# Skipped expert pairs counted before the used ones: blocks numbered from the end, norm work split four and four

## The reference

```python
def modulated_norm(x, g, shift, scale):
    return rmsnorm(x, g) * (1 + scale) + shift

def hierarchical_moe(h, wg, bg, we, be, w1, w3, w2):
    pg = softmax(x @ wg + bg);  pg_sel, g_sel = top_k(pg, 1)          # one of 4 groups
    le_sel = (x @ we + be) of that group                              # 4 experts in it
    w_top, i_top = top_k(softmax(le_sel), 2)                          # two experts
    w_top = w_top / sum(w_top) * pg_sel
    hid = silu(x @ w1[e]) * (x @ w3[e]);  y = sum_e gates[e] * (hid @ w2[e])
```

## Time and profile before

| | us |
|---|---|
| median of 3 runs | 2230.29 (2224.9 to 2230.62) |
| profiled execution, its own time | 2219.47 |
| its span in the trace | 2217.3 |
| PE busy | 1915.4 (86%) |
| DVE busy | 896.2 (40%) |
| ACT busy | 481.3 (22%) |
| POOL busy | 373.1 (17%) |

### The profile page before, as it was taken

One profiled execution on the slowest core, in us unless ns is written; L12 is line 12 of the kernel. 1 busy time (PEld: TensorE's weight loads), 2 busy tenths in 40 slices (PEclk: granted clock), 3 DMA queues, 4 the chain that ended last, 5 costly groups with the idle time before them and its releaser, 6 DMA issues. The chain is left out here.

```text
span 2217.3 us, 24642 instructions
## 1 busy us (share of the span) xinstructions
PE 1915.4 (86%) x9669; PEld 1300.0 (59%) x9669; DVE 896.2 (40%) x1686; ACT 481.3 (22%) x810; POOL 373.1 (17%) x280
## 2 busy tenths in 40 slices
PE   3899978978888895899679999888888889599975
PEld 2455655558888754444345566556888865444433
DVE  2179014565555424011237920546555541311114
ACT  1211013351111213122131101344111120322212
POOL 0001150043433102100111000005444300300001
PEclk8999897999999997899789999899999999699996
DMA  9322896800000003999562112530000000499953
GB/s 358 41 75 82 278 290 209 298 1 1 1 1 1 10 2 129 354 364 365 218 161 76 38 57 77 197 126 1 1 1 1 1 12 0 168 383 358 372 226 121
DMA packets 113920, 302.54 MB, mean 136 GB/s; under 512 B 27904, under 2 KB 35746, under 8 KB 100642
## 3 DMA queue, kind: packets, MB, share of 16 engines
q1 hardware_dynamic: 65424, 218.73, 26.7%
q0 software_dynamic: 14080, 53.48, 7.3%
q10 hardware_dynamic: 34322, 28.99, 4.6%
HBM read 235.09 MB, written 67.05 MB: 136 GB/s over the span
## 5 line engine op out<-in xcount | busy, mean ns | idle before, releaser
L626 PE MATMUL ps<-hreg,ring 128*128 128x512 f32 x768 | 400.2, 603 | 7.7 <-ACT hreg L1141 7.7
L627 PEld LDWEIGHTS ps<-hreg,ring 128*128 128x128 f32 x768 | 147.8, 192 | 187.6 <-issue 187.6
L986 PE MATMUL ps<-ring,tok 128*128 128x512 f32 x544 | 237.9, 595 | 0.2 <-issue 0.2
L986 PEld LDWEIGHTS ps<-ring,tok 128*128 128x128 f32 x544 | 103.9, 191 | 130.9 <-issue 130.9
L627 PE MATMUL ps<-hreg,ring 128*128 128x128 f32 x768 | 149.0, 276 | 0.0
L1969 POOL TENSOR_TENSOR hreg<-hreg,cst 128x512 f32<-128x512 f32 x70 | 88.9, 1270 | 301.7 <-DVE hreg L1674 254.7
L1001 PE MATMUL ps<-ring,work 128*128 128x512 f32 x272 | 123.7, 598 | 0.0
L626 PEld LDWEIGHTS ps<-hreg,ring 128*128 128x128 f32 x768 | 118.8, 195 | 8.0 <-issue 8.0
L1881 DVE TENSOR_TENSOR work<-work,ps 128x256 f32<-128x256 f32 x34 | 14.2, 421 | 252.5 <-ACT work L1364 252.5
L1503 DVE SCALAR_TENSOR_TENSOR mixA<-cin_reg,small,mixA 128x655 f32<-128x655 f32 x120 | 107.0, 895 | 0.0
L1687 DVE TENSOR_TENSOR hreg<-hreg,ps 128x512 f32<-128x512 f32 x50 | 34.3, 687 | 164.9 <-PE ps L846 164.9
(11 more groups left out here) (358 smaller groups left out, 3306.5 us busy)
## 6 DMA issues: line engine op xcount, KB each, us to landing
ring<-in_w SPq DMA_DIRECT2D x102, 1024.0 KB, 8.2
ring<-in_w_mod SPq DMA_DIRECT2D x24, 2048.0 KB, 8.6
ring<-in_w_in SPq DMA_DIRECT2D x12, 2048.0 KB, 9.0
ys<-zs ACTq DMA_DIRECT2D x34, 512.0 KB, 7.8
tok<-xs SPq DMA_DIRECT2D x30, 512.0 KB, 11.0
xs<-zero POOLq DMA_DIRECT2D x8, 1792.0 KB, 19.6
ys<-zero POOLq DMA_DIRECT2D x8, 1664.0 KB, 18.6
ring<-in_w_out SPq DMA_DIRECT2D x4, 2048.0 KB, 8.1
```

What stands on the lines that cost most here:

```text
L626: mm(o[:, 0:TS], lhs(k), rhs(k)[:, 0:TS], start=k == 0, stop=k == nk - 1)
L627: ins = mm(o[:, TS:T], lhs(k), rhs(k)[:, TS:T], start=k == 0, stop=k == nk - 1)
L986: ins = mm(bank(2 + q), xgT[q][:, k, :], w, start=k == 0, stop=k == KD - 1)
```

## The change

Four things are done.

1. The experts' blocks are shifted behind the unused ones: with skip = 26 - 2 x (used pairs), each slot moves up by 128 x skip rows and each expert's end by skip blocks. In every engine's loop the branch is turned round: pairs below skip / 2 raise their semaphores, the rest do the work. In SP's loop, which starts at pair 1 and has a limit of its own (skip + 2), the raises have lost their waits.
2. The norm's eight chunks are split four (DVE) and four (POOL), and all of DVE's stand ahead of the selection. ACT takes the chunks in order.
3. The bias row is spread over all partitions by two small products in the output projection (m == 2) and copied by DVE (m == 3); the logits then need one product per chunk, and DVE adds the bias as it reads them.
4. Block 1 is turned into other PSUM banks (`turn_block(1, 2048)`), without the wait for ACT's copy of block 0.

The second block's expert is computed for itself (entry NBLK + 2 of `blocks`). The order of the transfers in SP's and POOL's streams is the same in both kernels.

```diff
-                e = sp.value_load(blocks[0:1, 1:2], min_val=0, max_val=NE - 1)
+                e = sp.value_load(blocks[0:1, NBLK + 2:NBLK + 3], min_val=0, max_val=NE - 1)
                 up_load(1, e)
                 down_load(1, e)
                 need(xs_written, 16 * 2 * NCH)
-                in_use = sp.value_load(blocks[0:1, NBLK:NBLK + 1], min_val=1, max_val=NBLK)
+                unused = sp.value_load(blocks[0:1, NBLK + 1:NBLK + 2], min_val=2, max_val=NBLK + 2)
                 with sp.Fori(1, NPAIR) as pr:
-                    with sp.If(pr * 2 < in_use):
+                    with sp.If(pr * 2 < unused):
+                        for q in range(2):
+                            sp.sem_inc(ring_loaded[q], 32)
+                            sp.sem_inc(w2_loaded[q].sem, 16)
+                            sp.sem_inc(xg_loaded[q].sem, 16)
+                    with sp.Else():
...
-                need(xg_copied, 1)
                 need(xf_loaded[1], 16)
-                turn_block(1)
+                turn_block(1, 2048)
...
-                with act.Fori(0, NPAIR) as pr:
-                    with act.If(pr * 2 < in_use):
-                        pair(pr)
-                    with act.Else():
+                with act.Fori(0, NPAIR) as pr:
+                    with act.If(pr * 2 < unused):
                         for sig, n in ((sil_ready, 0), (xg_copied, 2), (hid_copied, 0)):
                             wait(pr, sig, n, 2)
                             act.sem_inc(sig.sem, 2)
                         for q in range(2):
                             wait(pr, ys_stored[q], 0, 16)
                             act.sem_inc(ys_stored[q].sem, 16)
+                    with act.Else():
+                        pair(pr)
...
-                norm_one(0)
+                for k in range(4):
+                    norm_one(k)
...
-                norm_one(1)
-
...
-                V.tensor_copy(slots[:, :], sl).then_inc(slots_ready.sem, 1)
...
+                step(V.tensor_tensor(t3, end[:, NE - 1:NE].to_broadcast([P, NPAIR]),
+                                     cst[:, C_BLK:C_BLK + NBLK].rearrange("p (n a) -> p a n", a=2)[:, 0, :], ALU.is_gt))
+                step(V.tensor_reduce(used, t3, AX, ALU.add))
+                step(V.tensor_scalar(skip, used, -2.0, float(NBLK), ALU.mult, ALU.add))
+                V.tensor_scalar(bf[:, NBLK + 1:NBLK + 2], skip, 2.0, None, ALU.add)
+                step(V.tensor_scalar(used, skip, float(P), None, ALU.mult))
+                V.tensor_scalar(slots[:, :], sl, used, None, ALU.add).then_inc(slots_ready.sem, 1)
+                step(V.tensor_scalar(wide_[:, 32:32 + NE], end, 1.0, None, ALU.is_le))
+                step(V.tensor_reduce(bf[:, NBLK + 2:NBLK + 3], wide_[:, 32:32 + NE], AX, ALU.add))
+                step(V.tensor_scalar(end, end, skip, None, ALU.add))
...
-                for k in range(2, KD):
+                for k in range(4, KD):
                     G.tensor_tensor(hT[:, k, :], xT[:, k, :], rst, ALU.mult).then_inc(norm_xp.sem, 1)
```

More of the change, by code:

```diff
@@ L212, in build @@
         crow = work[0:2, 512:532]
+        crb = work[:, 752:852].rearrange("p (c n) -> p c n", c=NCH)
         route_c = work[:, 544:544 + NX]
@@ L538, in _ @@
                             down_load(q, experts[q])
-                    with sp.Else():
-                        for q in range(2):
-                            sp.wait_ge(ring_loaded[q], up_base[l][q] + pr * 32)
-                            sp.sem_inc(ring_loaded[q], 32)
-                            sp.wait_ge(w2_loaded[q].sem, w2_loaded[q].at(l, 0) + pr * 16)
-                            sp.sem_inc(w2_loaded[q].sem, 16)
-                            sp.wait_ge(xg_loaded[q].sem, xg_loaded[q].at(l, -16) + pr * 16)
-                            sp.sem_inc(xg_loaded[q].sem, 16)
             sp.wait_ge(once["y_stored"], 32)
@@ L918, in _ @@
                         ins.then_inc(logit_rows.sem, 1)
+                    if m == 2:
+                        need(logit_copied, 1)
+                        for g_ in range(2):
+                            ins = mm(ps[:, 2940 + 20 * g_:2960 + 20 * g_], ident[0:2, g_:g_ + 1].to_broadcast([2, P]), crow,
+                                     start=True, stop=True)
+                        ins.then_inc(logit_rows.sem, 1)
                 need(mod2_ready, 2)
@@ L1037, in _ @@
                             pe.sem_inc(sig.sem, 2)
+                    with pe.Else():
+                        pair(pr)
                 need(xg_copied, NBLK + 2)
@@ L1132, in norm @@
                     sh = 24 * n
-                    for k in range(KD) if n == 0 else (0, 2, 3, 4, 1, 5, 6, 7):
+                    for k in range(KD):
                         if n == 0:
                             need(norm_x, k + 1)
-                        elif k < 2:
+                        elif k < 4:
                             need(norm_x, KD + k + 1)
                         else:
-                            need(norm_xp, k - 1)
+                            need(norm_xp, k - 3)
                         A_(hT[:, k, 0:TS], hT[:, k, 0:TS], ACT.Identity, scale=A[n][:, k, 0:1], bias=mod[:, sh + k, 0:1])
@@ L1372, in _ @@
                 copy_tokens(0, 0)
-                copy_tokens(0, 1)
+                copy_tokens(0, 1, 2048)
                 if l + 1 < L:
@@ L1888, in _ @@
                 dve.sem_inc(once["turns"], 1)
-                in_use = dve.value_load(blocks[0:1, NBLK:NBLK + 1], min_val=1, max_val=NBLK)
+                unused = dve.value_load(blocks[0:1, NBLK:NBLK + 1], min_val=0, max_val=NBLK)
                 with dve.Fori(0, NPAIR) as pr:
-                    with dve.If(pr * 2 < in_use):
-                        pair(pr)
-                    with dve.Else():
+                    with dve.If(pr * 2 < unused):
                         for sig in (hid_ready, y_out):
@@ L1897, in _ @@
                             dve.sem_inc(sig.sem, 2)
+                    with dve.Else():
+                        pair(pr)
                 def weigh(c_):
```

44 lines of the change are left out of this document (23 added, 21 removed).

## The result

The changed kernel takes **2249.31 us** (median of 5 runs, 2244.11 to 2253.52), the kernel before 2230.29 (5 runs, 2224.9 to 2231.36): a ratio of **1.0093, 95% interval 1.0073 to 1.0113**. It is slower by 0.9%, 19 us by the medians; 2251 was forecast, in a range of 2237 to 2259. Run again later beside other kernels on another chip, it gave 2250.19 us and a ratio of 1.0120 (1.0094 to 1.0145), which is 25 us by the medians: the size of the loss is known to about 5 us, its direction is not in doubt.

The account below looks back on a forecast made before the run. PE was taken as the busiest engine, so changes elsewhere count only where PE waits. Layer starts +14.3 and +14.1, projection +0.2, layer ends -7.6 gave +21 us on 2230.29: 2251 us, range 2237 to 2259.

Parts of the forecast that it names:

- ACT's gate in layer 0: Start of layer 0's experts: PE's first product waits for ACT's fifth skipped round, starting at 910.7 instead of 893.91 us.
- End of the layer: End of each layer: gathers no longer wait for ACT's skipped rounds, saving 4.4 us in layer 0, 3.2 in layer 1.
- Routing: Norm and routing: turns of h start 2.2 us early, scatter lands 1.5 us sooner, block 1's turn ends 3.1 early.
- SP's gate in layer 1: Start of layer 1's experts: PE's first product waits for SP's skipped rounds, starting at 1953.5 instead of 1941.45 us.
- The clock: First expert products: PE, idle before, runs at a lower clock, losing 2.3 us more in layer 0, 2.1 in layer 1.
- Sum: Whole kernel: 14.3 + 14.1 + 0.2 - 7.6 = +21 us against the kernel before.
- (a): Rival, chance 0.07: at the experts' start only PE's own skipped rounds delay its first product; sum 0, 2230 us.
- (b): Rival, chance 0.05: skipping at the experts' start is wholly hidden under block 1's turn; 13.8 us saved, 2216 us.
- (c): Rival, chance 0.05: skip branches at the experts' start wait for code while DMA is full; +13 us more, 2264 us.
- (d): Rival, chance 0.03: blocks stay or another number of pairs is skipped; only the routing part counts, -4 us.
- the base: Whole kernel: profiled 2219.47 us plus 10.8 to the median of the runs, 2230.29, to which +21 was added.

Follow-up runs that it names:

- the shorter wait: Kernel before, with GpSimd's gathers waiting only for the stores of the used pairs, no renumbering: 2221.84 us, ratio 0.9974.
- two edits: Changed kernel with SP's raises in a loop ahead of its scatter wait and ACT's parameter loads behind its expert loop: 2231.07 us, ratio 1.0015.

## Why the prediction was right

Taken in the order of its steps; times are against the start of the routing, which was 1.02 us later in the changed kernel's trace. The mechanism came out as forecast, ACT's gate in layer 0 and SP's in layer 1; its terms were each off by about a microsecond.

- **End of the layer, -4.4 and -3.2 us.** From the second pair to the gather the changed kernel takes 164.95 us against 169.39, and 187.79 against 190.97: -4.44 and -3.18. Run by itself, the shorter wait gave the same.
- **Routing.** The products of VectorE end at 857.8, 856.8 without the shift (forecast 856.9); the chain to the selection's product on PE stands at 862.98, forecast 862.1 + 1.0. The turns of h come at 865.55, 2.6 us early where 2.2 was forecast, the first gathers at 877.84, 2.7 early instead of 2.2, SP's load of the count behind the scatter at 903.9 (before 903.4), which is 0.5 early and not 1.5. The second block is turned at 892.0, forecast 890.6 + 1.0.
- **ACT's gate in layer 0.** First branch 907.7 (forecast 908.8 - 3.1 + 1.0 = 906.7), and a round of 1.2 us where 1.1 was taken from the end of the layer. Together 1.6 us: PE starts 18.4 us later, forecast +16.8. One reason for the late branch is that the loads took 14.6 us, where the row read for the forecast had 14.0.
- **SP's gate in layer 1.** +10.9 us, forecast +12.1: SP's load of the count came 2.4 us earlier against the routing, and 1.5 was taken.
- **The clock.** The first 32 products took 16.22 us instead of 14.63, +1.6, and 16.93 instead of 14.81, +2.1; forecast +2.3 and +2.1. ACT's wait went and the down projection is back to 3.60 us, as forecast.
- **Sum.** Layer 0 +10.6 (forecast 14.3 - 4.4 = 9.9), layer 1 +9.9 (14.1 - 3.2 = 10.9), together +20.5; forecast +20.8, and +21 with the two products in the output projection.

**The rivals.** (a), PE's own rounds alone, is not what the change does, but it is what two edits made of it: 1.0015, where it gave a sum of 0; PE's own rounds are the next gate behind those of ACT and SP. It had the first products 4.8 and 3.4 us later than before, and they came 6.2 and 3.4 us later, with rounds of 1.75 and 1.9 us where it had taken 1.55. (b), the skip under PE's entry, fell with the first product's idle time of 21.28 us. (c) gave 2.6 us for each branch while DMA is full. The row that the forecast held against it was no test, since DMA was idle there: a share of 0.00 from 1086.5 to 1090.9 us in the kernel before. Nor are ACT's deciding rounds, at 0.12. PE's rounds are: at a share of 1.03 they took 1.75 us, 0.2 more than at the end of the layer and far from 2.6, and ACT's rounds in layer 1, at the same share, took 1.1. So the fetch that the Trainium skill (Runtime: NRT & Kernel Launch, instruction fetch mechanics) gives for a taken branch out of the loaded pages does not show for these branches at the price of (c); whether they left the loaded pages, no run here shows, and what makes PE's rounds longer stays open. (d) is out by the counts: five raises of ACT's x 3 and of SP's x 2 in the rows above are the five skipped pairs. What the Trainium skill (SBUF — State Buffer, on the shared port) says, that a VectorE operation with two SBUF inputs and a GpSimd operation that reads SBUF block each other for a whole instruction, agrees with this trace: six of the eight products took 2.1 us, the first of each engine 1.52 and 1.53.

What hit by cancelling, and not by being exact: +1.6 at ACT's gate against -1.2 at SP's, and -0.7 for the clock. And the base: the forecast added the 10.8 us between the profiled execution of before and its median without giving a reason. The column between the layers shows that most of them lie outside the mixtures: 802.65 us in that trace against 808.9 to 814.7 in the others. Last, by the second measurement of the changed kernel (1.0120, or 21 to 32 us) the +21 sits at the lower edge; that the first one met it to 2 us is in part chance.

## What to carry to other kernels

A skipped round of a run-time loop is not free (1.0 to 1.9 us on ACT, SP and PE here): moving such rounds from the end of a stage to its start pays where nothing waits at the start, and there PE waited for three engines' counts at once. Ask of a raise who needs it and from when on: a wait that counts only the used work (GpSimd's, here) saves the same time without moving anything. And an engine's queue of housekeeping DMAs (17 parameter loads, 14.6 us) can hold up the loop behind it, above all once an edit upstream makes the others earlier; but look where it lands when it is moved. Put on top of the gathers it cost 1.4 to 2.8 us, put 3.9 us behind the first of them it cost nothing that shows.

## What the runs showed of the chip that was not expected

- The price of a skipped round differs by engine and place, and it does not follow how full DMA is. ACT with 5 raises: 1.2 us at the start of the experts in layer 0 (DMA share 0.12), 1.1 in layer 1 (about 1.0) and at the end of the layer (0.00). SP with 6 raises and no waits: 1.2 us in layer 0 and 1.0 in layer 1. PE with 4 raises: 1.75 and 1.9 us at the start (1.03), 1.55 at the end. The causes are open.
- The 17 small loads, issued together with the gathers of the experts' outputs, went with gathers that took 7.9 to 8.1 us to land instead of 5.2 to 6.1, in all four traces in which they met.
- The stretch between the layers took 808.9 to 814.7 us in eleven traces and 802.65 in one. In the projection's tail the granted clock of 1299 to 1340 us was 0.85 in the changed kernel's trace and 0.88 in that of the kernel before, but 0.79 to 0.90 in the others without an order that an edit explains; what sets it is open.

```profile
1299.00:1340.00 41.00, 41.00 (x182) 27.94 (x181) 0.20 (x1) 2.59 (x5) 0.00 (x0) 0.88 0.15 52
```

```profile
1299.00:1340.00 41.00, 41.00 (x178) 29.45 (x177) 2.78 (x6) 3.77 (x7) 0.00 (x0) 0.85 0.15 52
```

The two rows are the view by stretches, before and changed; the last three columns are clock, DMA share and GB/s.
